# Ring slots of the streamed operand 4 bytes further apart, stationary buffers at multiples of 64 bytes

## What is computed

```
h = x + 1/2 * SwiGLU_1(norm(x))              # 2048 -> 2 x 5632 -> 2048
z = norm(h) @ W_mix_in                       # 2048 -> 5120, five groups of 1024
h = h + concat(y_conv, y_gmlp) @ W_mix_out   # 2048 -> 2048
h = h + XAttn(norm(h), norm(mem))            # w_q, w_k, w_v, w_o: 2048 -> 2048 each, 4 heads, 256 memory tokens
h = h + 1/2 * SwiGLU_2(norm(h))
out = norm_final(h)
```

## The kernel before

| buffer | role | start modulo 256 |
|---|---|---|
| w_hi, w_lo (every slot) | streamed | 128 |
| xT_hi, xT_lo | stationary (streamed in the scores) | 128 |
| hidT, yT, memT, v_hi, v_lo | stationary | 32 |
| pT_hi, pT_lo | streamed | 32 |

## Time and profile before

### The profile page before, as it was taken

One profiled execution on the slowest core, in us unless ns is written; L12 is line 12 of the kernel. 1 busy time (PEld: TensorE's weight loads), 2 busy tenths in 40 slices (PEclk: granted clock), 3 DMA queues, 4 the chain that ended last, 5 costly groups with the idle time before them and its releaser, 6 DMA issues.

```text
span 2187.2 us, 25558 instructions
## 1 busy us (share of the span) xinstructions
PE 2167.1 (99%) x9626; PEld 1778.9 (81%) x9626; DVE 1349.3 (62%) x1549; ACT 991.6 (45%) x1103; POOL 1.8 (0%) x7
## 2 busy tenths in 40 slices
PE   8999999999999999999999999999999999999998
PEld 6888888888888888888888888888888888888886
DVE  5676667666474547865677554576676667664544
ACT  5444454444343444444554444454444444443433
POOL 0000000000000000000000000000000000000000
PEclk9999999999999999999999999999999999999999
DMA  6666666665556565665556445466666666665553
GB/s 227 209 190 197 195 191 188 197 195 189 188 171 204 181 191 181 195 227 175 180 170 207 155 159 169 157 212 197 193 191 193 192 192 190 195 194 187 188 188 135
DMA packets 159217, 412.20 MB, mean 188 GB/s; under 512 B 12588, under 2 KB 13732, under 8 KB 158756
## 3 DMA queue, kind: packets, MB, share of 16 engines
q1 hardware_dynamic: 157728, 410.04, 60.2%
q10 hardware_dynamic: 1412, 1.11, 0.2%
HBM read 409.01 MB, written 2.10 MB: 188 GB/s over the span
## 4 chain that ended last, share of the span: by engine, by line
PE 96%; DVE 2%; ACT 1%; DMA 0%; issue 0%; ACTq 0%; DVEq 0%
PE ps L906 94%; PE ps L935 1%; DVE w_lo L575 1%; PE ps L919 1%; DVE ps L635 1%; DVE convT L748 0%; DVE xT_lo L583 0%; DMA h<-in_x 0%; ACT convT L444 0%; PE ps L1023 0%; ACT xT_hi L329 0%; ACT w_hi L321 0%; DVE stage L738 0%; ACT scratch L555 0%; ACT zT L441 0%
## 5 line engine op out<-in xcount | busy, mean ns | idle before, releaser
L575 DVE TENSOR_TENSOR w_lo<-raw,w_hi 128x1024 fp32r<-128x1024 f32 x768 | 936.1, 1224 | 773.8 <-ACT w_hi L321 768.6
L321 ACT ACTIVATE w_hi<-raw 128x1024 fp32r<-128x1024 f32 x768 | 811.8, 1061 | 1106.0 <-PE ps L906 1087.0
L906 PE MATMUL ps<-w_hi,xT_hi 128*128 128x512 f32 x1856 | 573.8, 390 | 5.3 <-DVE w_lo L575 5.3
L906 PE MATMUL ps<-w_lo,xT_hi 128*128 128x512 f32 x1856 | 572.2, 389 | 0.0
L906 PE MATMUL ps<-w_hi,xT_lo 128*128 128x512 f32 x1856 | 572.0, 389 | 0.0
L906 PEld LDWEIGHTS ps<-w_hi,xT_hi 128*128 128x128 f32 x1856 | 347.8, 188 | 78.9 <-issue 4.1
L906 PEld LDWEIGHTS ps<-w_lo,xT_hi 128*128 128x128 f32 x1856 | 349.0, 188 | 72.7
L906 PEld LDWEIGHTS ps<-w_hi,xT_lo 128*128 128x128 f32 x1856 | 348.7, 188 | 72.8
L906 PE MATMUL ps<-w_hi,hidT_hi 128*128 128x512 f32 x704 | 223.5, 397 | 0.4 <-DVE w_lo L575 0.4
L906 PE MATMUL ps<-w_hi,hidT_lo 128*128 128x512 f32 x704 | 222.7, 395 | 0.0
L906 PE MATMUL ps<-w_lo,hidT_hi 128*128 128x512 f32 x704 | 221.3, 393 | 0.0
(11 more groups left out here) (119 smaller groups left out, 800.7 us busy)
## 6 DMA issues: line engine op xcount, KB each, us to landing
raw<-in_w_ffn_in SPq DMA_DIRECT2D x352, 512.0 KB, 4.1
raw<-in_w_ffn_out SPq DMA_DIRECT2D x176, 512.0 KB, 4.3
raw<-in_w_mix_in SPq DMA_DIRECT2D x80, 512.0 KB, 4.2
raw<-in_w_mix_out SPq DMA_DIRECT2D x32, 512.0 KB, 3.7
raw<-in_w_xq SPq DMA_DIRECT2D x32, 512.0 KB, 3.8
raw<-in_w_xk SPq DMA_DIRECT2D x32, 512.0 KB, 3.9
raw<-in_w_xv SPq DMA_DIRECT2D x32, 512.0 KB, 3.6
raw<-in_w_xo SPq DMA_DIRECT2D x32, 512.0 KB, 3.6
```

The costliest lines, as they stand in the source:

```text
L321: nc.scalar.activation(w_hi[:, k % RING, :], raw[:, k % RAW, :], ACT.Copy).then_inc(hi_ready, 1)
L575: nc.vector.tensor_tensor(w_lo[:, k % RING, :], raw[:, k % RAW, :], w_hi[:, k % RING, :].bitcast(F32), ALU.subtract).then_inc(lo_ready, 1)
L906: ins = nc.tensor.matmul(bank(s, t * GW + b * BLK, BLK), xs[:, k, t * P:(t + 1) * P], ws_[:, k % RING, b * BLK:(b + 1) * BLK], start=(k == ...
```

## The change

It moves buffers and nothing else: no instruction, wait or transfer is added, removed or reordered. The function `lane` raises an address to a wanted place modulo 256. `w_hi` and `w_lo` become flat, with slots of 1025 elements (4100 bytes) of which 1024 are used.

```diff
+    PITCH = 256
+    def lane(at, to):
+        return at + (to - at) % PITCH

     h = put("h", [P, TOK, D], F32)
+    place["at"] = lane(place["at"], 0)
     xT_hi = put("xT_hi", [P, KD, SEQ], F32R)
     xT_lo = put("xT_lo", [P, KD, SEQ], F32R)
     raw = put("raw", [P, RAW, GW], F32)
-    w_hi = put("w_hi", [P, RING, GW], F32R)
-    w_lo = put("w_lo", [P, RING, GW], F32R)
+    SKEW = 1
+    SLOT = GW + SKEW
+    place["at"] = lane(place["at"], 0)
+    w_hi_ring = put("w_hi", [P, RING * SLOT], F32R)
+    place["at"] = lane(place["at"], 0)
+    w_lo_ring = put("w_lo", [P, RING * SLOT], F32R)
+    w_hi = [w_hi_ring[:, i * SLOT:i * SLOT + GW] for i in range(RING)]
+    w_lo = [w_lo_ring[:, i * SLOT:i * SLOT + GW] for i in range(RING)]
...
-    big = extra + 8 * KB
+    big = lane(extra + 8 * KB, 64)
...
-    yT_hi = put("yT_hi", [P, KD, SEQ], F32R, at=big)
+    yT_hi = put("yT_hi", [P, KD, SEQ], F32R, at=big + 64)
...
-    memT_hi = put("memT_hi", [P, KD, SEQ], F32R, at=big + 32 * KB)
+    memT_hi = put("memT_hi", [P, KD, SEQ], F32R, at=big + 128 + 32 * KB)
...
-                    nc.scalar.activation(w_hi[:, k % RING, :], raw[:, k % RAW, :], ACT.Copy).then_inc(hi_ready, 1)
+                    nc.scalar.activation(w_hi[k % RING], raw[:, k % RAW, :], ACT.Copy).then_inc(hi_ready, 1)
...
-                                                       ws_[:, k % RING, b * BLK:(b + 1) * BLK],
+                                                       ws_[k % RING][:, b * BLK:(b + 1) * BLK],
```

More of the change, by code:

```diff
@@ L142, in build @@
     g_fin = put("g_fin", [P, D], F32, at=extra)
-    big = extra + 8 * KB
+    big = lane(extra + 8 * KB, 64)
     hidT_hi = put("hidT_hi", [P, KF, SEQ], F32R, at=big)
     hidT_lo = put("hidT_lo", [P, KF, SEQ], F32R, at=big + KF * KB)
-    yT_hi = put("yT_hi", [P, KD, SEQ], F32R, at=big)
-    yT_lo = put("yT_lo", [P, KD, SEQ], F32R, at=big + 16 * KB)
-    memT_hi = put("memT_hi", [P, KD, SEQ], F32R, at=big + 32 * KB)
[L149 to L159, removed]
+    yT_hi = put("yT_hi", [P, KD, SEQ], F32R, at=big + 64)
+    yT_lo = put("yT_lo", [P, KD, SEQ], F32R, at=big + 64 + 16 * KB)
+    memT_hi = put("memT_hi", [P, KD, SEQ], F32R, at=big + 128 + 32 * KB)
+    memT_lo = put("memT_lo", [P, KD, SEQ], F32R, at=big + 128 + 48 * KB)
+    c_buf = put("c_buf", [P, TOK, GW], F32, at=big + 128 + 32 * KB)
+    zT = put("zT", [P, HALF, SEQ], F32, at=big + 128 + 40 * KB)
+    convT = put("convT", [P, HALF, SEQ], F32, at=big + 128 + 48 * KB)
+    v_buf = put("v_buf", [P, TOK, GW], F32, at=big + 128 + 56 * KB)
+    wsT = put("wsT", [P, HEADS, P], F32, at=big + 128 + 64 * KB)
+    sg = put("sg", [P, TOK, GW], F32, at=big + 128 + 80 * KB)
+    mem_nat = put("mem_nat", [P, TOK, D], F32, at=big + 128 + 64 * KB)
+    v_hi = put("v_hi", [P, TOK, GW], F32R, at=big + 128 + 64 * KB)
+    v_lo = put("v_lo", [P, TOK, GW], F32R, at=big + 128 + 72 * KB)
+    pT_lo = put("pT_lo", [P, XA_HEADS * 2, SEQ], F32R, at=big + 128 + 80 * KB)
     qT_hi, qT_lo = yT_hi, yT_lo
     kT_hi, kT_lo = xT_hi, xT_lo
-    assert big + 2 * KF * KB <= nc.sbuf_usable_end
+    assert big + 128 + 2 * KF * KB <= nc.sbuf_usable_end
     vectors = [("g_ffn1", g_ffn1[0], KD), ("g_mix", g_mix[0], KD), ("g_xattn", g_xattn[0], KD), ("g_mem", g_mem[0], KD),
@@ L574, in lo_units @@
                     dve.wait_ge(hi_ready, unit0 + (k + 1))
-                    nc.vector.tensor_tensor(w_lo[:, k % RING, :], raw[:, k % RAW, :], w_hi[:, k % RING, :].bitcast(F32),
+                    nc.vector.tensor_tensor(w_lo[k % RING], raw[:, k % RAW, :], w_hi[k % RING].bitcast(F32),
                                             ALU.subtract).then_inc(lo_ready, 1)
```

## The result

The changed kernel takes 2220.3 us (2219.59 to 2221.0), against 2189.39 us before: a ratio of 1.014 [1.0121, 1.0159], 1.4% slower, where 1.0% faster was forecast. The time lies inside the range; the direction is wrong.

The account below looks back on a forecast made before the run. TensorE bounds the kernel, matmul count times pace: 2189.4 - 24.3 (stationary buffers) - 1.3 (256-column matmuls) + 2.9 (streamed tiles) = 2166.7 us, 1.0% faster, counted as the same. The range was 2156 to 2260 us.

Parts of the forecast that it names:

- What bounds the kernel: TensorE, busy 99% of the span: time is the number of matmuls times the pace of one; producers run ahead.
- Stationary buffers to multiples of 64: All 3648 matmuls on hidT, yT and memT go from 233.3 to 226.7 ns, 24.3 us less.
- Streamed tiles at 0, 4, 8 and 12: 6912 matmuls in three slots of four start unaligned; one cycle, 0.42 ns, more each, 2.9 us in all.
- Rival A: Unaligned stream pays as the stationary operand does, 16 cycles per matmul in slots 1 to 3; 2209.9 us; chance 0.17.
- Rival B: Unaligned stream pays a cycle more per 64 bytes, 2256 us, or per 16 bytes, 2532 us; chance 0.20.
- Rival C: Staggered slots undo a conflict with the weight load; pace falls at most to 213.3 ns, 2041 us; chance 0.06.
- half form: Half of the conflict's 122.9 us goes, besides the 24.3 us for the stationary buffers; 2104 us.
- The 256-column matmuls: 192 matmuls, scores and with the probabilities, gain 0 to 6.67 ns each; 1.3 us less counted.
- Transposes: Their buffers stage, scratch and ident move to 32 past a multiple of 64; no cost, 0 taken.
- ScalarE and VectorE: Writing and reading the shifted slots costs VectorE at most 3 ns, ScalarE has no row; 0 taken.

Follow-up runs that it names:

- all_zero: Changed kernel without the skew, every stationary buffer and streamed slot at 0 modulo 256; 2165.53 us, ratio 0.989 to the kernel before.
- lanes_only: Changed kernel with slots of 1024 elements again, so the new buffer places without the skew; 2185.04 us, ratio 0.998 to the kernel before.
- distance_16: Changed kernel without skew, streamed slots at 16 modulo 256, xT and yT at 32, hidT 0, memT 64; 2235.82 us, ratio 1.0211 to the kernel before.
- slots_64: Changed kernel with stationary buffers at 0 modulo 256 and slots of 1040 elements, starting at 0, 64, 128, 192; 2204.26 us, ratio 1.007 to the kernel before.
- both_off_4: Changed kernel without skew, streamed slots and xT at 4 modulo 256, hidT 0, yT 32, memT 64; 2248.35 us, ratio 1.0267 to the kernel before.
- both_32: Changed kernel without skew, streamed slots and xT at 32 modulo 256, hidT 64, yT 96, memT 128; 2189.16 us, ratio 0.9999 to the kernel before.

## Why the prediction was wrong, step by step

- *What bounds the kernel.* Right. The time is the count of matmuls times the pace; TensorE's wait for VectorE was 4.7 us, against 5.7, and each run's time follows from its paces. `all_zero` confirms the sum itself: 2189.4 - 24.3 - 1.3 = 2163.8 was what the text gave without the skew, and 2165.5 was measured once all distances were 0.
- *Stationary buffers to multiples of 64: the step that failed first.* I read the 16 cycles of `hidT`, `yT` and `memT` as the price of their 32 bytes, 24.3 us to win. The rows fitted two readings, and I chose "a half line off" over "a distance of 0 for `xT` alone", which I had named as the lower bound. `lanes_only` gives 4.3 us in all, and beside the skew even that is gone. Nearly all of the 24.3 us was there to be had, at distance 0 (`all_zero`: 23.9).
- *Streamed tiles at 0, 4, 8 and 12: the term that was mis-sized.* I took 0.42 ns per shifted matmul, 2.9 us. Next to `lanes_only` the skew costs 35.3 us, and alone 28.1. On `xT` the slots pay 5, 25, 15 and 11 cycles, 14 on the mean, 5.8 ns x 5568 = 32 us; the other 3 us are `memT`, from 549 to 560. The row that I rested it on, `pT` streamed 32 bytes off, had a stationary operand at the same place (distance 0) and 256 columns, where the runs show other prices; it said nothing about 4 bytes.
- *Rival A* had 16 cycles in slots 1 to 3 and was nearest in size, but not in place: the shifted units pay 11 to 25, slot 0 pays 5 in its first matmuls after the change of slot, and `hidT` pays nothing on the mean, being at 560 already. With the 4.3 us in place of the 24.3, its sum would have been 2189.4 - 4.3 - 1.3 + 46.1 = 2229.9. That the measured time lies inside the range comes from the bounds that A and B gave, not from the forecast's own terms.
- *Rival B*, a cycle per 64 or 16 bytes, would be 32 or 128 cycles in each of slots 1 to 3. Only slot 1 came near the first: 25 on `xT`, and on `memT` 570 to 576 against 549; slots 2 and 3 did not. *Rival C*, that staggering would undo a conflict, had the sign wrong: no buffer or slot had a mean pace under 544, to a tenth of a cycle. (Its half form, by the terms of the sum, is 2163.8 - 61.4 = 2102 and not 2104.)
- *The 256-column matmuls.* The four blocks of 48 take 5.70 or 5.75 us each after, 5.75 before: 0.1 us in all, a tenth of the 1.3 us counted. *Transposes.* Right: a block of 16 takes 1.75 us before and after. *ScalarE and VectorE.* Right, 1061 and 1225 ns.

What stays open: why the pace depends on the two starts. Shown is that the distance modulo 256 goes with it when the streamed tiles start at 0, 32 or 128 and all slots alike (`distance_16`, streamed at 16, does not fit in); that with a start at 4 on either side nothing runs at 544 cycles; and that neither the length of the weight load nor the number of columns alone carries the price. Whether a start at 4 costs by itself or by the distance that it makes is open. The paces repeat in patterns, often of two or three matmuls (231 and 236 ns in turn on `hidT` in `lanes_only`), so two reads that fall into step would fit, but no run isolates them. A dependence on the place modulo 512 does not show in the aligned layouts: in `all_zero`, by the addresses in its kernel, `xT` starts a multiple of 512 bytes from both rings and the other three 256 bytes off one, and all take 544 to 545 cycles; in `slots_64` `xT` and `hidT` differ in the same way and agree to 0.1 cycle in the settled pace of three slots and to 0.3 in the fourth. Yet something beyond the start modulo 256 counts elsewhere: in `both_off_4` slot 0 runs at 560 cycles and the others at 565, though all slots start at the same place modulo 4096, and `xT` and `yT` differ in `distance_16`. What the matmuls before leave behind was not separated from it.

## What to carry to other kernels

When TensorE bounds a kernel and its fp32r matmuls are further apart than their columns explain, look at where the operands start: give all stationary buffers and all streamed slots the same start modulo 256, a multiple of 32, and don't pad ring slots by an element. Here that is worth 1.1% against the kernel before and 2.5% against the skewed one, with no instruction changed; for other shapes and types measure it, since at 256 columns the order of the placements turned. A difference between two groups that differ in two properties needs one run for each property before a gain is booked on either.

## What the runs showed that was not expected

- A matmul's pace depends on the pair of starts: 544 cycles at distance 0, 558 at 4, 560 at 32 and 64, 562 at 96, 558 at 128, 549 at 192 (streamed tiles at 0, or at 32 in `both_32`; the value at 4 has a stationary start off a multiple of 16 too).
- In the changed kernel the slot that starts at 4 is the slowest with every stationary buffer (566 to 570 cycles on the mean, 576 on `memT` once settled); on `xT`, a start at 8 costs less (559) and one at 12 less again (555).
- With fewer stationary columns, and so shorter weight loads, the matmuls on `xT` were slower: 544 cycles with 128, 552 with 64, 556 with 32.
- A change of slot is felt for five matmuls and more: in the changed kernel slot 0, itself at distance 0, starts a unit at 228 to 236 ns and reaches 227 after the fifth.
